# One wait less ahead of the load of expert 0's down weights, in a two-layer trunk step with a mixture of experts

## The chip, the cores and the metric

The kernel runs on one core of a Trainium2 chip. The metric is the device time of one execution in microseconds; of several executions the median is taken. Inside a core, TensorE (PE) multiplies matrices, VectorE (DVE) and ScalarE (ACT) work element by element, GpSimd (POOL) does small work and issues the indirect DMAs, and SyncE (SP) does nothing but wait and issue loads. All DMAs of a core, whoever issues them, are carried by its 16 DMA engines.

## What is computed

Two layers, each of attention (three groups of heads) and a mixture of experts, for 128 context tokens and 256 latent tokens, 384 in all, of width 1024. The change lies where the mixture of experts begins:

```python
def moe(h, w_router, b_router, w_gate, w_up, w_down):
    ...
    scores = jax.nn.sigmoid(jnp.einsum('nd,de->ne', t, w_router, ...))
    ...                                   # the best group of 4, then the top 2 in it
    hg = jnp.einsum('nd,edf->nef', t, w_gate)      # 16 experts, 1024 -> 512
    hu = jnp.einsum('nd,edf->nef', t, w_up)
    a = jax.nn.silu(hg) * hu * gate[..., None].astype(t.dtype)
    y = jnp.einsum('nef,efd->nd', a, w_down)       # 512 -> 1024
```

The kernel does not compute all 384 tokens for each of the 16 experts: it gathers the tokens that chose an expert, multiplies them with that expert's three matrices, and scatters the rows back.

## The kernel before

**Weights.** Every weight matrix of an expert (gate, up, down) is 2 MB in float32. SP loads them, in the order in which they are wanted, into a ring of six SBUF slots (`ring`). Each layer reuses the slots that held the attention weights and, last before the experts, chunks of the modulation matrix `w_ada`. In an expert phase SP's list is: gate 0 into slot 0, up 0 into slot 1, gate 1 into slot 2, up 1 into slot 3, down 0 into slot 4, gate 2 into slot 5, up 2 into slot 0 again, down 1 into slot 1, and so on, 48 loads in a layer. Gate 2 and what follows are read by number from `order`, a list of experts sorted by their token counts, which DVE writes in the router (L2398, semaphore `s_order`). `step(i, u)` (below) issues the three loads that go with expert 2i+1+u: its gate and up and the down matrix of the expert before it. Ahead of each load SP waits until the slot is free: the first time for the last reader of what stood in it (`before(slot)`, `is_filled`, L574), later for PE to have used up the expert's weights (`s_gd`, `s_gu`, `s_y`).

**Tokens.** In the router ACT writes the rows of the normalised activations to a scratch tensor in HBM (`hscr`, three DMAs of 512 KB from L1749). DVE makes the row numbers of the first two experts (`idx`, L2378), and POOL gathers their tokens from `hscr` (L2735), expert 0 first, then expert 1. PE turns expert 0's tokens (`tokens(0, ...)`, L1308), ACT and DVE split them into a high and a low part, and the matmuls of gate 0 start.

**Splitting the weights.** Weights in heavy experts are multiplied as a rounded high part and a remainder: ACT writes the high part (L1765), DVE the low part (L2437), and PE runs three matmuls per block (L1231, L1232, L1239). Half of the experts (those with few tokens) are "light" and are multiplied as they are (L1326, L1328, L1261). The loop over the experts is the same on every engine, in a fixed order per engine, so an engine that waits for a piece holds up all that stands behind it in its own list.

**The wait in question** stands in `step`, ahead of the down load of expert 0, so once in each layer: SP waits until the semaphore of the even gathers has risen by 16, that is, until expert 0's tokens lie in SBUF. It stands ahead of the check of slot 4, and gate 2 into slot 5 comes behind it on the same queue.

Of the kernel before, what the change touches and what calls it, by code (L numbers as in the profile page):

```python
# [263 lines left out]
def build(nc, A, C_dram, O):  # L264
    with ExitStack() as ctx:
# [389 lines left out]
        def gathers(l, p):  # L655

            return (s_g, [l * k for k in G_PASS]) if p == 0 else (s_gf[l, p], [0, 0])
# [25 lines left out]
        def _(sp):  # L683
# [4 lines left out]
            def chunk(l, k, parts):  # L688
                slot = k % SLOTS

                if k >= SLOTS:
                    is_filled(sp, last_reader(l, k - SLOTS))
                elif l > 0:
                    ring_after_experts(sp, slot, PASSES * (l - 1) + 1)
                for dst, src in parts(ring[slot][:]):
                    sp.dma_start(dst, src).then_inc(s_land[slot], 16)

            def cols(w, c, n):
                def parts(r):
                    return [(r[:, 0:KT * n].rearrange("p (k n) -> p k n", k=KT),  # L700
                             w.rearrange("(k p) n -> p k n", p=P)[:, :, c:c + n])]
                return parts

            def in_tail(l):

                w = A["w_in"][l].rearrange("(k p) n -> p k n", p=P)
                a = NA_IN + QR
                b = a + KR + RD + SH * HD

                def parts(r):  # L710
                    v = r[:, 0:KT * 416].rearrange("p (k n) -> p k n", k=KT)
                    return [(v[:, :, 0:KR + RD], w[:, :, a:a + KR + RD]), (v[:, :, KR + RD:416], w[:, :, b:b + 256])]
                return parts

            def in_swq(l):

                w = A["w_in"][l].rearrange("(k p) n -> p k n", p=P)
                a = NA_IN + QR + KR + RD

                def parts(r):  # L720
                    v = r[:, 0:KT * 384].rearrange("p (k h s d) -> p k h s d", k=KT, h=3, s=2)
                    return [(v[:, :, h, s, :], w[:, :, a + (3 * s + h) * HD:a + (3 * s + h + 1) * HD])
                            for h in range(3) for s in range(2)]
                return parts

            def out_cols(l, c):

                w = A["w_out"][l]
                a = 5 * P
                b = a + SH // 2 * HD  # L730

                def parts(r):
                    v = r.rearrange("p (k n) -> p k n", k=KT)
                    return [(v[:, 0:5, :], w[0:a].rearrange("(k p) n -> p k n", p=P)[:, :, c:c + 512])] + \
                           [(v[HD * s:HD * (s + 1), 5:8, :], w[r0:r0 + SH // 2 * HD].rearrange("(k p) n -> p k n", p=HD)[:, :, c:c + 512])
                            for s, r0 in enumerate((a, b))]
                return parts

            for l in range(DEPTH):
                w_in = (cols(A["w_in"][l], 0, 512), cols(A["w_in"][l], 512, 512), in_tail(l), in_swq(l))  # L740
                for k, (kind, *x) in enumerate(STREAM[l]):
                    if (l, k) == (0, len(ADA_FIRST) + 1):
                        sp.dma_start(cst[:, 2 * P:], C_dram[:, 2 * P:KEPT_W]).then_inc(s_const2, 16)
                        sp.dma_start(swaf, C_dram[:, KEPT_W:CONST_W]).then_inc(s_swaf, 16)
                    if kind in ("rows", "none"):
                        continue
                    if kind == "ada":
                        chunk(l, k, cols(A["w_ada"][x[0]], x[1] * 512, 512))
                    elif kind == "in":
                        chunk(l, k, w_in[x[0]])  # L750
                    else:
                        chunk(l, k, out_cols(l, x[0] * 512))

                def load(l, p, slot, use, w, e):
                    src = w[l, e] if isinstance(e, int) else w[l, bass.ds(e, 1)].rearrange("a p n -> (a p) n")
                    sp.dma_start(ring[slot][:], src).then_inc(moe_land(l, p, slot, 0)[0], 16)

                def stream(p):
                    n = PASSES * l + p

                    def before(slot):

                        if p == 0:
                            is_filled(sp, last_reader(l, MOE_AT[l] - SLOTS + slot))
                        else:
                            ring_after_experts(sp, slot, n)
                    before(0)
                    load(l, p, 0, 0, wg_d, 0)
                    before(1)
                    load(l, p, 1, 0, wu_d, 0)  # L770

                    def expert_at(e):

                        if p or (isinstance(e, int) and e < 2):
                            return e
                        at_e = order[0:1, e:e + 1] if isinstance(e, int) else order[0:1, bass.ds(e, 1)]
                        return sp.value_load(at_e, min_val=0, max_val=NE - 1)

                    def step(i, u):

                        e = 2 * i + 1 + u
                        if p == 0 and isinstance(i, int) and (i, u) == (0, 1):
                            sp.wait_ge(s_order, l + 1)
                        here, back_one = expert_at(e), expert_at(e - 1)
                        for kind, (w, s, back) in enumerate(((wg_d, s_gd, 1), (wu_d, s_gu, 1), (wd_d, s_y, 2))):
                            slot, use = place(u, kind)
                            if p == 0 and isinstance(i, int) and (e, kind) == (1, 2):
                                sp.wait_ge(gathers(l, 0)[0][0], gathers(l, 0)[1][0] + 16)
                            if isinstance(i, int) and i == 0 and use == 0:
                                before(slot)  # L790
                            elif isinstance(i, int) and i == 0:

                                sp.wait_ge((s_gd, s_gu)[slot], n * NE + 1)
                            else:
                                sp.wait_ge(s, e + n * NE - back)
                            load(l, p, slot, use, w, back_one if kind == 2 else here)
                    step(0, 0)
                    step(0, 1)
                    with sp.Fori(1, NE // 2 - 1) as i:
                        step(i, 0)  # L800
                        step(i, 1)
                    step(NE // 2 - 1, 0)
                    last_one = expert_at(NE - 1)
                    sp.wait_ge(s_gd, n * NE + NE - 1)
                    load(l, p, 5, 0, wd_d, last_one)
                    if p:

                        sp.wait_ge(s_y, (n + 1) * NE)

                stream(0)  # L810

                sp.wait_ge(s_cnt, l + 1)
                most = sp.value_load(cnti[0:1, 0:1], min_val=0, max_val=T)

                def rows_back(passes):

                    if passes == 1:
                        sp.wait_ge(s_gu, NE * PASSES * l + NE - 1)
                        sp.wait_ge(s_y, NE * PASSES * l + NE - 2)
                    else:  # L820
                        sp.wait_ge(s_y, NE * PASSES * (l + 1))
                        sp.wait_ge(s_further, (PASSES - 1) * (l + 1))
                    for k in range(2):
                        sp.wait_ge(s_sc[k], (l + 1) * SC_FIRST)
                    for t in range(NT):
                        sp.dma_start(yl[t], yscr.rearrange("(k t p) d -> t p k d", k=TOPK, p=P)[t]).then_inc(s_yl[t], 16)

                def skip_streams(p, many):
                    rows_back(p)
                    for s in s_land2:  # L830
                        wait(sp, s, 16 * (MOE_CH // SLOTS) * ((PASSES - 1) * l + p - 1))
                        for _ in range(many):
                            sp.sem_inc(s, 16 * MOE_CH // SLOTS)

                def stream_and_rows(p):
                    stream(p)
                    if p == PASSES - 1:
                        rows_back(PASSES)

                further_passes(sp, most, stream_and_rows, skip_streams)  # L840
# [1986 lines left out]
```

## Time and profile before

| | us |
|---|---|
| three runs | 1092.69, 1094.74, 1096.26 |
| median of the runs | 1094.74 |
| the profiled execution, its own time | 1095.41 |
| its span, first to last instruction | 1093.4 |
| mean granted TensorE clock over the span | 0.978 |

The profile's span is 2.0 us shorter than the time of that execution; the rest lies around the program. The profiled execution is 0.67 us above the median of the runs. PE is busy for 1008.0 us of the span (92%), DVE for 649.6 us, ACT for 534.3 us and POOL for 184.1 us; the queue that carries SP's loads moved 285.58 MB. Layer 0's expert phase lies at about 277 to 545 us of the span, layer 1's at about 794 to 1065 us.

Each row read from the trace below is a whole line of an answer. In a timeline a row gives start and duration of an instruction, the engine, the line of the kernel, what it writes and reads, and, in square brackets, how long the engine stood idle before it and what ended that.

### The profile page before, as it was taken

How to read it: one execution, taken by the hardware profiler on the slowest of the kernel's cores; microseconds unless marked ns; L12 is line 12 of the kernel's file. 1: busy time of each engine (PE TensorE's matmuls, PEld its weight loads, DVE VectorE, ACT ScalarE, POOL GpSimd, SP SyncE). 2: the span in 40 equal slices, each digit the busy share in tenths (PEclk: the TensorE clock that was granted, in tenths of full speed). 3: DMA queues.
4: the chain of work that ended last, by engine and by line, in shares of the span. 5: the costliest groups of instructions: out<-in, count | busy, mean ns of one | idle time of the engine just before them, and what ended most of it. 6: DMA issues, size and time to landing. Idle time of an engine off the chain costs nothing.

```text
span 1093.4 us, 15340 instructions
## 1 busy us (share of the span) xinstructions
PE 1008.0 (92%) x5607; PEld 699.0 (64%) x5607; DVE 649.6 (59%) x1135; ACT 534.3 (49%) x809; POOL 184.1 (17%) x184
## 2 busy tenths in 40 slices
PE   6999998897899999999999999789789999999987
PEld 4799454594686666665549975459368666666545
DVE  4355645667996454555345546775799644455534
ACT  2423554635575444555324356663646554445523
POOL 0226200150121111221040011000023111122002
PEclk8999999999899999999989999999989999999998
DMA  9997998347699999999699463002779999999961
GB/s 347 345 331 213 360 304 285 109 149 289 242 353 366 416 414 414 422 390 414 266 382 277 152 206 120 1 2 77 289 260 380 372 411 413 415 411 402 407 246 58
DMA packets 80895, 320.03 MB, mean 293 GB/s; under 512 B 20755, under 2 KB 25217, under 8 KB 68028
## 3 DMA queue, kind: packets, MB, share of 16 engines
q1 hardware_dynamic: 67232, 285.58, 68.7%
q0 software_dynamic: 12496, 30.37, 8.3%
q10 hardware_dynamic: 1100, 3.23, 0.7%
q8 instruction: 37, 0.61, 0.2%
q14 instruction: 30, 0.25, 0.1%
HBM read 304.38 MB, written 27.43 MB: 303 GB/s over the span
## 4 chain that ended last, share of the span: by engine, by line
PE 61%; DMA 14%; DVE 11%; ACT 6%; issue 5%; SPq 1%; POOL 0%; ACTq 0%; DVEq 0%; POOLq 0%
DMA ring<-in_w_down 12%; PE bank L1239 7%; PE bank L1231 6%; PE bank L1232 6%; PE bank L1326 4%; PE bank L947 3%; PE bank L951 3%; PE bank L944 3%; PE bank L1124 2%; PE bank L1138 2%; PE bank L1261 2%; ACT work L1705 2%; DVE ring_r L2437 2%; PE bank L921 2%; ACT work_r L1765 2%
## 5 line engine op out<-in xcount | busy, mean ns | idle before, releaser
L2437 DVE TENSOR_TENSOR ring_r<-ring,work_r 128x4096 fp32r<-128x4096 f32 x52 | 228.7, 4419 | 59.4 <-ACT work_r L1765 59.2
L1765 ACT ACTIVATE work_r<-ring 128x4096 fp32r<-128x4096 f32 x51 | 185.2, 3632 | 43.6 <-DMA ring<-in_w_down 18.9
L1231 PE MATMUL bank<-work_r 128*128 128x512 f32 x432 | 172.6, 399 | 6.1 <-DVE work_r L2453 5.1
L1232 PE MATMUL bank<-work_r 128*128 128x512 f32 x432 | 168.6, 390 | 0.0
L1239 PE MATMUL bank<-ring_r,work_r 128*128 128x512 f32 x432 | 112.0, 401 | 4.3 <-DVE ring_r L2437 4.3
L2735 POOL DMA_INDIRECT work<-hscr,idx x32 | 56.0, 1751 | 330.7 <-PE bank L1317 98.6
L1326 PE MATMUL bank<-ring,work 128*64 128x512 f32 x224 | 99.1, 595 | 0.0
L1328 PE MATMUL bank<-ring,work 128*64 128x512 f32 x224 | 99.1, 595 | 0.0
L1231 PEld LDWEIGHTS bank<-work_r 128*128 128x128 f32 x432 | 81.2, 188 | 26.6 <-issue 7.3
L1239 PEld LDWEIGHTS bank<-ring_r,work_r 128*128 128x128 f32 x432 | 79.2, 188 | 28.8 <-DVE ring_r L2437 11.6
L1232 PEld LDWEIGHTS bank<-work_r 128*128 128x128 f32 x432 | 81.2, 188 | 16.2
L2746 POOL DMA_INDIRECT yscr<-work,idx x28 | 39.1, 1396 | 187.6 <-ACT work L1831 121.1
L1326 PEld LDWEIGHTS bank<-ring,work 128*64 128x64 f32 x224 | 29.5, 137 | 57.7 <-issue 56.0
L1621 ACT ACTIVATE work_r<-ring 128x512 fp32r<-128x512 f32 (+1 forms) x48 | 28.8, 605 | 68.4 <-PE bank L951 68.3
L2089 DVE TENSOR_TENSOR ring_r<-ring,work_r 128x512 fp32r<-128x512 f32 (+1 forms) x48 | 33.1, 696 | 48.7 <-ACT work_r L1621 48.6
L2480 DVE TENSOR_TENSOR work_r<-bank,work_r 128x512 fp32r<-128x512 f32 x18 | 12.4, 691 | 81.2 <-ACT work_r L1817 81.2
L921 PE MATMUL bank<-ring,sil 128*32 128x512 f32 x384 | 52.0, 665 | 9.3 <-ACT work L1705 6.3
L1261 PE MATMUL bank<-ring,work 128*64 128x512 f32 x224 | 54.0, 627 | 6.6 <-issue 6.6
L1705 ACT ACTIVATE work<-bank,st 128x384 f32<-128x384 f32 (+1 forms) x96 | 47.9, 506 | 19.2 <-DVE st L2180 10.8
L2180 DVE TENSOR_REDUCE st<-bank 128x2 f32<-128x768 f32 (+1 forms) x48 | 37.3, 778 | 29.5 <-PE bank L1124 19.7
L1771 ACT ACTIVATE work<-bank 128x512 f32<-128x512 f32 x14 | 8.4, 598 | 79.2 <-PE bank L1317 79.2
L1124 PE MATMUL bank<-work 64*128 64x384 f32 (+3 forms) x192 | 45.6, 453 | 0.9 <-ACT work L1705 0.9
(307 smaller groups left out, 1743.4 us busy)
## 6 DMA issues: line engine op xcount, KB each, us to landing
ring<-in_w_gate SPq DMA_DIRECT2D x32, 2048.0 KB, 14.6
ring<-in_w_up SPq DMA_DIRECT2D x32, 2048.0 KB, 16.9
ring<-in_w_down SPq DMA_DIRECT2D x32, 2048.0 KB, 17.9
ring<-in_w_ada SPq DMA_DIRECT2D x24, 2048.0 KB, 11.2
ring<-in_w_in SPq DMA_DIRECT2D x4, 2048.0 KB, 19.0
yscr<-hT POOLq DMA_DIRECT2D x2, 3072.0 KB, 13.1
ring<-yscr SPq DMA_DIRECT2D x6, 1024.0 KB, 7.3
ring<-in_w_out SPq DMA_DIRECT2D x4, 1280.0 KB, 6.3
```

The costliest lines, as they stand in the source:

```text
L921: last = mm(b[32 * (k % 4):32 * (k % 4) + 32, :], sil32[:, k, :], w[:, k, :], start=(k < 4), stop=(k >= 4), skip_group_check=True)
L1124: last = mm(b[:, s, 0:n], lhs, rhs, start=True, stop=True)
L1231: mm(b[:], x_hi[:, k, :], hi[:, k, half, :], start=(k == 0), stop=False)
L1232: last = mm(b[:], x_lo[:, k, :], hi[:, k, half, :], start=False, stop=False)
L1239: last = mm(b[:], x_hi[:, k, :], lo[:, k, half, :], start=False, stop=(k == nk - 1))
L1261: last = mm(b[LS * h:LS * h + LS, :], aT[:, k, :], w[:, k, h, :], start=(k == 0), stop=(k == 3), skip_group_check=True)
L1326: up = mm(bG[0:LS, :], xs_l[:, k, :], wu[:, k, 0, :], start=(k == 0), stop=(k == KT - 1), skip_group_check=True)
L1328: gate = mm(bG[LS:P, :], xs_l[:, k, :], wg[:, k, 0, :], start=(k == 0), stop=(k == KT - 1), skip_group_check=True)
L1705: ins = A_(pr[(2 * i + s) % 6][:, 0:n], b[:, s], ACT.Exp, bias=st[:, r, 0, s:s + 1], accum_out=st[:, r, 1, s:s + 1])
L1765: A_(w_hi[:, slot % 2, :], ring[slot][:], ACT.Copy).then_inc(s_hi, 1 + behind)
L2437: tt(ring_r[slot][:], ring[slot][:], w_hi[:, slot % 2, :].bitcast(F32), ALU.subtract).then_inc(s_lo, 1 + behind)
L2735: g.indirect_dma_start(grow[rows, e % 2, :], None, hscr, bass.IndirectOffsetOnAxis(ap=idx[rows, e + 2, 0:1], axis=0), bounds_check=bound_h ...
```

## The change

The wait is taken out, in both layers. Nothing else differs: order of the loads, slots, and all other waits are the same.

```diff
@@ -784,8 +784,6 @@
                         here, back_one = expert_at(e), expert_at(e - 1)
                         for kind, (w, s, back) in enumerate(((wg_d, s_gd, 1), (wu_d, s_gu, 1), (wd_d, s_y, 2))):
                             slot, use = place(u, kind)
-                            if p == 0 and isinstance(i, int) and (e, kind) == (1, 2):
-                                sp.wait_ge(gathers(l, 0)[0][0], gathers(l, 0)[1][0] + 16)
                             if isinstance(i, int) and i == 0 and use == 0:
                                 before(slot)
                             elif isinstance(i, int) and i == 0:
```

With e = 1 and kind = 2 the load is `wd_d` of `back_one`, which is expert 0.

## Rows read from the trace of the kernel before

**Rows 1.** The page's part 4: the chain that ended last, by engine, by line.
```profile
PE 61%; DMA 14%; DVE 11%; ACT 6%; issue 5%; SPq 1%; POOL 0%; ACTq 0%; DVEq 0%; POOLq 0%
DMA ring<-in_w_down 12%; PE bank L1239 7%; PE bank L1231 6%; PE bank L1232 6%; PE bank L1326 4%; PE bank L947 3%; PE bank L951 3%; PE bank L944 3%; PE bank L1124 2%; PE bank L1138 2%; PE bank L1261 2%; ACT work L1705 2%; DVE ring_r L2437 2%; PE bank L921 2%; ACT work_r L1765 2%
```

**Rows 2.** Windows of layer 0: length, busy by engine, PE clock, DMA share, GB/s.
```profile
293.00:294.00 1.00, 1.00 (x9) 0.92 (x8) 0.86 (x6) 1.00 (x1) 0.00 (x0) 1.00 0.10 33
...
301.00:302.00 1.00, 1.00 (x6) 0.84 (x5) 1.00 (x1) 0.68 (x1) 1.00 (x1) 1.00 0.00 0
...
345.00:346.00 1.00, 1.00 (x10) 0.95 (x10) 1.00 (x1) 1.00 (x2) 0.00 (x0) 1.00 0.27 103
346.00:440.00 94.00, 94.00 (x438) 59.95 (x437) 48.58 (x31) 48.98 (x43) 14.90 (x13) 1.00 1.01 413
```

**Rows 3.** Windows of layer 1: the same columns.
```profile
817.00:818.00 1.00, 1.00 (x6) 0.82 (x5) 1.00 (x1) 1.00 (x1) 1.00 (x1) 1.00 0.04 16
```

**Rows 4.** Waits of SP's queue, 260:300 and 780:815: us in total, times, longest.
```profile
SPq L756 <- DMA work<-hscr,idx: 10.9, 1, 10.9
...
SPq L756 <- DMA work<-hscr,idx: 13.0, 1, 13.0
```

**Rows 5.** Timeline of SP: down 0, gate 2, up 2 (layer 0); down 0 (layer 1).
```profile
280.48 0.33 SPq L756 DMA_DIRECT2D ring<-in_w_down  x1
281.86 0.36 SPq L756 DMA_DIRECT2D ring<-in_w_gate  x1
293.46 0.34 SPq L756 DMA_DIRECT2D ring<-in_w_up  x1
...
798.33 0.33 SPq L756 DMA_DIRECT2D ring<-in_w_down  x1
```

**Rows 6.** Landing of one load with the DMA engines to itself, issued at 748.1.
```profile
DMA to landing us min/median/max: 7.8/7.8/7.8
```

**Rows 7.** Line L1749, the three writes of hscr: layer 0, then layer 1.
```profile
L1749 ACTq DMA_DIRECT2D hscr<-work x3: 327/350/362, 267.1 to 270.1; - x3
...
DMA to landing us min/median/max: 2.8/3.1/3.3
...
L1749 ACTq DMA_DIRECT2D hscr<-work x3: 327/328/1147, 782.9 to 786.7; - x3
...
DMA to landing us min/median/max: 3.0/4.1/4.3
```

**Rows 8.** Timeline of POOL: the first gather of layer 0, of layer 1.
```profile
277.07 1.10 POOL L2735 DMA_INDIRECT work<-hscr,idx  x1 [40.63 <-DVE idx L2378]
...
794.12 1.09 POOL L2735 DMA_INDIRECT work<-hscr,idx  x1 [63.04 <-issue]
```

**Rows 9.** Timeline of DVE: order (layer 0); row numbers, order (layer 1).
```profile
278.49 0.19 DVE L2398 CAST order<-ranked 128x14 int32<-128x14 f32 x1
...
793.14 0.17 DVE L2378 TENSOR_SCALAR idx<-slotf 128x4 int32<-128x4 f32 x1
...
795.60 0.17 DVE L2398 CAST order<-ranked 128x14 int32<-128x14 f32 x1
```

**Rows 10.** Landing, line L2735: first gather layer 0, layer 1; second, layer 0; all 32.
```profile
DMA to landing us min/median/max: 3.4/3.4/3.4
...
DMA to landing us min/median/max: 4.2/4.2/4.2
...
DMA to landing us min/median/max: 4.4/4.4/4.4
...
DMA to landing us min/median/max: 3.4/9.0/14.7
```

**Rows 11.** Timeline of PE: expert 0's tokens turned, layer 0 and layer 1.
```profile
281.99 1.92 PE L1308 MATMUL bank<-cst,work 128*128 128x128 f32 x8
...
800.61 1.04 PE L1308 MATMUL bank<-cst,work 128*128 128x128 f32 x8
```

**Rows 12.** Timeline of ACT: the first use of down 0, layer 0.
```profile
307.63 3.63 ACT L1765 ACTIVATE work_r<-ring 128x4096 fp32r<-128x4096 f32 x1
```

## The prediction

> **What bounds the kernel now.** I began with the chain that ended last, because the change touches loads only: if loads sit on that chain, an earlier load may pay. PE has 61% of it, and one kind of load, the down weights, has 12%, the largest single line [rows 1]. So loads matter somewhere; the question is whether they matter where this load stands. Next I read the windows of the expert phase. In layer 0, from 346 to 440 us, the 16 DMA engines are full (share 1.01, 413 GB/s) and PE is busy for all 94.00 us [rows 2]: both run flat out. But before that there are stretches in which the DMA engines have nothing left to carry: share 0.10 in 293 to 294, 0.00 in 301 to 302 and 0.27 in 345 to 346 [rows 2]; in layer 1, 0.04 in 817 to 818 [rows 3]. PE is busy for the whole of each of these windows. What the reader should see: the stream of loads runs dry several times after the place of the change, while PE goes on working. A stream that runs dry forgets when its earlier parts were delivered. Last I read the waits of SP's queue: the gather held it for 10.9 us in layer 0 and 13.0 us in layer 1, once each [rows 4]. That is the wait that goes, 23.9 us in total, and it is a wait of SP alone.
>
> **The change part by part.**
>
> *Down 0 moves forward.* It is issued at 280.48 and at 798.33 [rows 5]. Without the wait it goes when slot 4 is free, which is where the wait for the gather began to count: 280.48 - 10.9 = 269.6 in layer 0, 798.33 - 13.0 = 785.3 in layer 1. A load that has the engines to itself lands 7.8 us after its issue [rows 6], so at 277.4 and 793.1. What runs beside it are the writes of hscr, the last issued at 270.1 and 786.7 [rows 7]; each is 0.52 MB, 1.3 us at 413 GB/s [rows 2]. At most two of them are still under way, so down 0 lands between 277.4 and 280.0, and between 793.1 and 795.7.
>
> *What that buys.* The first instruction that reads down 0 is ACT's split at 307.63 in layer 0, and no wait stands before it in its row [rows 12]; ACT starts it when its own work before it is through. Down 0 had been issued 27 us earlier and has 27 us to land even now. Nothing is bought here: 0 us. The cover is those 27 us, against 7.8 us that a load needs; if the cover were gone, the worth would be the transfer, up to 5.1 us (2.1 MB at 413 GB/s).
>
> *Gate 2 moves forward a little.* It stands behind down 0 and needs `order`, which is written at 278.49 + 0.19 = 278.68 in layer 0 and 795.60 + 0.17 = 795.77 in layer 1 [rows 9]. Between down 0 and gate 2 on SP lie 281.86 - 280.48 = 1.38 us [rows 5], of which 0.33 is down 0's own issue, so some 1.05 us go into reading the expert's number. Gate 2 then goes at about 279.7 (2.2 us earlier) and, by the same distance, at about 796.8. It is used after down 0, so it too was early enough: 0 us.
>
> *All the loads behind these do not move.* Up 2 is issued at 293.46 [rows 5] into slot 0, which PE must first have used up. The DMA engines stand nearly still in 293 to 294 [rows 2], so up 2 meets an empty stream before and after the change, and from it on every load has its old issue time. The transfer of down 0 is taken out of the stretch between 280.48 and 293.46 and put before it; what it leaves behind is a longer hole ahead of up 2. What is late next is still PE.
>
> *What stands in the way of the moved load: the writes of hscr.* The first gather reads what they write. In layer 0 the last write lands at 270.1 + 3.3 = 273.4 at the latest, the gather starts at 277.07 and names DVE's row numbers as what it waited for [rows 7, 8]: 3.7 us to spare. In layer 1 it lands at 786.7 + 4.3 = 791.0 at the latest, the row numbers are there at 793.14 + 0.17 = 793.31 [rows 7, 9]: 2.3 us to spare. If the write and down 0 share the engines evenly, the write takes 1.3 us longer: covered. If the whole of down 0 went ahead of it, 5.1 us longer, the gather would start 1.4 us late in layer 0 and 2.8 us late in layer 1; the slack that follows (next paragraph) leaves 0 and 0.5 us of it. Bounds 0 and +0.5 us; I take 0, because the write and the load are different queues and only one of the two is 7.8 us long.
>
> *The issue of the writes on ACT.* One of the three issues in layer 1 took 1.147 us where the others took 0.33 [rows 7]; I can't tell from the trace why. Should down 0's issue at 785.3 slow the write at 786.7 in the same way, ACT is 0.8 us late once. Bounds from 0 to +0.8 us; I take 0. A gain is excluded, since nothing is taken from ACT's list.
>
> *The first gather itself.* It starts at 277.07 and 794.12 [rows 8] and lands 3.4 and 4.2 us later [rows 10], at 280.5 and 798.3. PE turns the tokens at 281.99 and 800.61 [rows 11], in both layers without idle time of its own named in the row. So the gather may land 1.5 us later in layer 0 and 2.3 us later in layer 1 before PE sees it. What is new beside it: the tail of down 0, which is over by 280.0 at the latest in layer 0 and by 795.7 in layer 1, and in layer 1 the first packets of gate 2, issued at about 796.8. The nearest row for a gather with a load beside it is the second gather of layer 0, which runs while down 0 starts: 4.4 us [rows 10], 1.0 us more than the first. The far end is the median of all 32 gathers, 9.0 us [rows 10], most of which run with the engines full. By the near row the delay is 1.0 us and covered; by the far end it costs 286.1 - 281.99 = 4.1 us and 803.1 - 800.61 = 2.5 us. I take the near row, 0 us, because down 0 is all but over when the gather begins.
>
> A rule speaks against the change here. The rows show a gather at 3.4 to 4.4 us in quiet engines and 9.0 us in the median. The Trainium skill (DMA: Bandwidth & Descriptors, section "Issuing engines are not separate DMA queues") says that transfers of all issuers run on the same 16 engines and interleave, so SP's load takes bandwidth from POOL's gather although the queues differ; this trace agrees as far as the 4.4 against 3.4 us go. By the rule alone the sum would rise by what the gather loses beyond its slack, which is the slower rival below.
>
> *Sum.* 0 + 0 + 0 + 0 us, with +0.5 + 0.8 us of small bounds and +6.6 us at the far end of the gather, nothing below zero except by the rival that follows. Against the profiled execution: 1095.41 + 0 = 1095.41. That execution is 0.67 us above the median of the runs, so the median I expect is 1094.7.
>
> **The rivals.**
>
> *Faster: the load stream is one queue, and 2.1 MB taken out of its busy part shortens it.* For: down loads are the largest line of the chain [rows 1], and from 346 us on the engines are full [rows 2]. If the stream were full from 281 us on, each layer would end 5.1 us earlier, 10.2 us in total: 1094.7 - 10.2 = 1084.5. Against: the three dry stretches in layer 0 and the one in layer 1 [rows 2, 3]; any lead is lost at the first of them. The Trainium skill (Perfetto Trace Analysis, section "Optimization Strategy") advises to look for the gaps on the most contended engine and to let what they wait for start sooner, which is just what this change does to the DMA engines; by that rule the gain would come, and the rows of the dry stretches speak against it here. Chance 0.05.
>
> *Slower: the first gather lands late.* The place is PE's turn of expert 0's tokens; it decides from the point at which the gather lands after 281.99 in layer 0 and 800.61 in layer 1. All later loads are issued when PE has used slots up, so a late PE makes a late stream, and the delay goes through to the end. Price at the median gather: 4.1 + 2.5 = 6.6 us, 1101.3. For: the wait kept every load off the engines just while this gather ran, and the gather's packets are few and needed to the last. Against: down 0 has 7.5 us (277.07 - 269.6) and 8.8 us (794.12 - 785.3) ahead of the gather, about what a load needs [rows 6]. Chance 0.10, half of it for a smaller loss of 1 to 4 us.
>
> *The change doesn't do what it says.* If something else holds SP at the same place (slot 4, or `order`, should it be read ahead of down 0), down 0 keeps its time. The split of SP's wait speaks against it: 10.9 and 13.0 us are put to the gather alone [rows 4]. The time would be 1094.7 as well. Chance 0.05, and it counts as no change.
>
> **How the numbers follow.** A measurement of this kernel can tell about 0.3%, 3.3 us, from no change; the three runs lie within 3.6 us. Forecast (no change because the moved transfer was off the chain): 0.80; with the idle change 0.85 in all, of which I give 0.05 to the two sides for noise and for the small bounds. Within 0.3%: 0.80. Faster: 0.05 + 0.02 = 0.07. Slower: 0.10 + 0.03 = 0.13. The likeliest time is 1094.7. The range takes the noise of the runs on the lower side, 1091.0, and on the upper side the small bounds and the smaller half of the late gather, 1099.5; the full price of either rival lies outside, about 1 in 10 together.
>
> **What would show each step.** In the profile of the changed kernel SP should issue down 0 at about 269.6 and 785.3 and gate 2 at about 279.7 and 796.8, and up 2 still at about 293.5; the wait for the gather should be gone from SP's list. The DMA share should rise in 271 to 278 and in 787 to 794, fall to nothing in about 287 to 294, and be as before from there on. The first gathers should land before 282.0 and 800.6, and L1308 should start within 0.3 us of its old times. The prediction is wrong if PE's first expert starts later (the gather, or the writes ahead of it), or if, with the same start, the stream from 302 us on runs ahead of the old one.

## The result, and the profile after

The median rose from 1094.6 (now of four runs) to 1106.56 us (1106.07 to 1107.51). The ratio is 1.0108, with a 95% interval from 1.0093 to 1.0123: 12 us slower, where I had forecast no change in a range from 1091.0 to 1099.5. The profiled execution took 1106.07 us; its span is 1104.0 us, 10.6 us more than before, at a mean clock of 0.975.

The moved loads did what the prediction said. The timeline of SP, after (down 0, gate 2, up 2 in both layers; it answers [rows 5]):

```profile
267.84 0.33 SPq L756 DMA_DIRECT2D ring<-in_w_down  x1
278.03 0.36 SPq L756 DMA_DIRECT2D ring<-in_w_gate  x1
297.42 0.34 SPq L756 DMA_DIRECT2D ring<-in_w_up  x1
...
787.72 0.33 SPq L756 DMA_DIRECT2D ring<-in_w_down  x1
798.12 0.35 SPq L756 DMA_DIRECT2D ring<-in_w_gate  x1
818.76 0.34 SPq L756 DMA_DIRECT2D ring<-in_w_up  x1
```

To read these against before, the drift of the execution has to be taken off. Up 1 is the last load ahead of the change. Its rows, and that of up 2 in layer 1 before; first after, then before:

```profile
253.47 0.33 SPq L756 DMA_DIRECT2D ring<-in_w_up  x1
...
772.13 0.33 SPq L756 DMA_DIRECT2D ring<-in_w_up  x1
```

```profile
255.14 0.33 SPq L756 DMA_DIRECT2D ring<-in_w_up  x1
...
769.72 0.33 SPq L756 DMA_DIRECT2D ring<-in_w_up  x1
...
809.96 0.34 SPq L756 DMA_DIRECT2D ring<-in_w_up  x1
```

Up 1 is issued 1.67 us earlier than before in layer 0 and 2.41 us later in layer 1. Up 2 is issued 297.42 - 293.46 = 3.96 us later in layer 0 and 818.76 - 809.96 = 8.80 us later in layer 1. So between up 1 and up 2 the kernel loses 3.96 + 1.67 = **5.6 us** in layer 0 and 8.80 - 2.41 = **6.4 us** in layer 1, 12.0 us in all. Every load of layer 0 from up 2 to the last ones near 512 us is 3.8 to 4.0 us late: the loss is made in these 40 us and is then carried along, neither given back nor added to; in layer 1 the loads from up 2 to 1028 us are 8.2 to 8.9 us late in the same way. (The difference of two up 2's, less that of two up 1's, is what "loss" means in the table below.)

In that stretch three things are late, one behind the other. The third write of hscr, after (groups by line, from its issue to its landing; answers [rows 7]; layer 0, then layer 1):

```profile
L1747 ACTq DMA_DIRECT2D hscr<-work x1: 326/326/326, 268.5 to 268.5; - x1
DMA to landing us min/median/max: 9.6/9.6/9.6
...
L1747 ACTq DMA_DIRECT2D hscr<-work x1: 326/326/326, 788.3 to 788.3; - x1
DMA to landing us min/median/max: 9.1/9.1/9.1
```

It is issued 0.6 us behind down 0 and takes 9.6 and 9.1 us, where it took 3.3 and 3.0 [rows 7]. The first gather of POOL and its landing, after (answers [rows 8, 10]):

```profile
278.91 1.56 POOL L2733 DMA_INDIRECT work<-hscr,idx  x1 [44.15 <-DMA hscr<-work]
DMA to landing us min/median/max: 7.6/7.6/7.6
...
797.68 1.09 POOL L2733 DMA_INDIRECT work<-hscr,idx  x1 [64.20 <-DMA hscr<-work]
DMA to landing us min/median/max: 9.4/9.4/9.4
```

The releaser in brackets has changed: the gather no longer starts on DVE's row numbers but on the write. The row numbers after (layer 0, layer 1), and before (layer 0; layer 1 is in [rows 9]):

```profile
274.37 0.17 DVE L2376 TENSOR_SCALAR idx<-slotf 128x4 int32<-128x4 f32 x1
...
794.68 0.17 DVE L2376 TENSOR_SCALAR idx<-slotf 128x4 int32<-128x4 f32 x1
```

```profile
276.02 0.17 DVE L2378 TENSOR_SCALAR idx<-slotf 128x4 int32<-128x4 f32 x1
```

They are there at 274.54 and 794.85, so the gather starts 4.4 and 2.8 us behind them, against 0.9 us (from 276.19) and 0.8 us before [rows 8, 9]. By then gate 2 is under way (278.03) or about to be (798.12), and the gather lands 7.6 and 9.4 us later instead of 3.4 and 4.2 [rows 10]: at 286.5 and 807.1, some 0.2 and 0.6 us after gate 2 itself (landing 8.3 and 8.4 us behind its issue). And PE, after (answers [rows 11]):

```profile
286.66 1.95 PE L1306 MATMUL bank<-cst,work 128*128 128x128 f32 x8 [7.45 <-DMA work<-hscr,idx]
807.16 1.97 PE L1306 MATMUL bank<-cst,work 128*128 128x128 f32 x8 [4.44 <-DMA work<-hscr,idx]
```

PE stands idle for 7.45 and 4.44 us for the gather, in front of expert 0's tokens, where its rows of before named no idle time. Less the drift, the turn of the tokens is 6.3 us late in layer 0 (286.66 - 281.99 + 1.67) and 4.1 us in layer 1 (807.16 - 800.61 - 2.41). In layer 1 another 2.3 us come before up 2. The windows there show the granted clock (the column behind the five engines), first after, then before:

```profile
802.00:806.00 4.00, 0.71 (x3) 0.00 (x1) 2.02 (x4) 0.00 (x0) 0.00 (x0) 0.93 0.87 360
806.00:810.00 4.00, 2.84 (x11) 2.15 (x12) 0.21 (x1) 0.84 (x2) 0.00 (x0) 0.50 0.12 50
810.00:814.00 4.00, 4.00 (x13) 2.69 (x12) 4.00 (x4) 0.25 (x1) 0.00 (x0) 0.67 0.01 4
```

```profile
802.00:806.00 4.00, 3.82 (x18) 2.60 (x17) 4.00 (x5) 0.78 (x2) 0.00 (x0) 1.00 1.00 426
806.00:810.00 4.00, 4.00 (x52) 3.29 (x51) 4.00 (x1) 2.86 (x1) 0.00 (x0) 1.00 0.94 397
```

Behind its idle stretch PE works at 0.50, the lower of its two levels (1.2 GHz), until past 810; before, it had the full clock here. That fits the 2.3 us; no run tested the clock by itself.

**Why the write is late.** The records of the DMA queues say it (queue, packets, MB, share of the 16 engines; q1 carries SP's loads, q10 ACT's writes), after, first in 270.3 to 272.7 us, then in 273 to 275.5:

```profile
q1 hardware_dynamic: 56, 0.92, 103.3%
...
q1 hardware_dynamic: 47, 0.77, 85.2%
q10 hardware_dynamic: 47, 0.19, 18.7%
```

Two things are to be seen. First, the write starts late. It was issued at 268.46, yet in this window of 2.4 us the load has the engines to itself (no packet of q10). By the records of single packets the write's first 4 KB row goes 4.5 us behind its issue, and 4.2 us in layer 1; in the kernel before it goes 0.8 us behind the issue in both. What holds it is open. Second, from 273 us on both queues get 47 packets in 2.5 us, one for one; but a load's packet is 16 KB and a packet of the write is one row of 4 KB, so the load gets four bytes for each byte of the write. The Trainium skill (DMA: Bandwidth & Descriptors, section "Queues, rings and completion order") says that each engine goes round between the queues it has work for, packet by packet. From 273 us on this trace agrees, 47 to 47 (the packets counted here are single rows); before that it shows 56 packets of the load to none of the write. Of the 6.3 us by which the write lands later than before in layer 0, some 3.7 us are the late start, and the rest, some 2.6 us, comes behind it, where the write takes turns with the longer packets.

The gather starts late in the same way. The queues after in layer 0 (q0 carries POOL's gathers), first in 279 to 283.8 us, then in 283.8 to 286.5:

```profile
q1 hardware_dynamic: 103, 1.69, 98.8%
...
q0 software_dynamic: 277, 0.26, 28.0%
```

Its first packet goes 4.9 us behind its start at 278.91 (5.2 us in layer 1), when most of gate 2 has been carried; in the kernel before it goes 1.7 us behind the start in both layers. So 3.2 and 3.5 of the 4.2 and 5.2 us by which the gather takes longer are the late start.

### The profile page after: what moved, and what is told of

It is laid out like the page before. It is cut to its first block, busy times and chain, and to the rows that moved or that the text cites. A ratio compares the mean times of both kernels' runs of the same rounds, so it can differ in the third digit from the quotient of the medians.

```text
span 1104.0 us, 15336 instructions
## 1 busy us (share of the span) xinstructions
PE 1006.0 (91%) x5605; PEld 697.4 (63%) x5607; DVE 649.0 (59%) x1135; ACT 534.4 (48%) x809; POOL 183.6 (17%) x184
## 4 chain that ended last, share of the span: by engine, by line
PE 60%; DMA 16%; issue 9%; DVE 7%; ACT 6%; SPq 1%; ACTq 0%; DVEq 0%; POOLq 0%
DMA ring<-in_w_down 12%; PE bank L1237 7%; PE bank L1229 6%; PE bank L1230 6%; PE bank L1324 5%; PE bank L1259 3%; PE bank L945 3%; PE bank L949 3%; PE bank L942 3%; PE bank L1122 2%; PE bank L1136 2%; ACT work L1703 2%; ACT work_r L1763 2%; DVE ring_r L2435 2%; PE bank L1014 2%
## 5 line engine op out<-in xcount | busy, mean ns | idle before, releaser
L2478 DVE TENSOR_TENSOR work_r<-bank,work_r 128x512 fp32r<-128x512 f32 x18 | 12.4, 691 | 81.2 <-ACT work_r L1815 81.2
L919 PE MATMUL bank<-ring,sil 128*32 128x512 f32 x384 | 49.6, 639 | 10.9 <-ACT work L1703 6.4
```

The costliest lines, as they stand in the source:

```text
L919: last = mm(b[32 * (k % 4):32 * (k % 4) + 32, :], sil32[:, k, :], w[:, k, :], start=(k < 4), stop=(k >= 4), skip_group_check=True)
```

## The experiments

The theory after reading: the third write is late because it takes turns with long packets (the turn theory; the late starts above are no part of it); the gather is then late and meets gate 2; PE's idle time is carried to the end (the chain theory). Rivals: that the early start of the loads in itself, whatever becomes of the gather, costs the time (a worse order in the stream, or loads beside other work); that the late write alone is the whole of it; that the meeting of gather and gate 2 alone is. In the kernels below, the same lines stand 2 to 6 lines lower down than in the one after.

| kernel | third write lands after, us | gather lands after, us | PE idle for the gather, us | loss, us | ratio to before |
|---|---|---|---|---|---|
| before | 3.3 / 3.0 | 3.4 / 4.2 | none / none | - | 1 |
| after | 9.6 / 9.1 | 7.6 / 9.4 | 7.45 / 4.44 | 5.6 / 6.4 | 1.0108 |
| gate 2 held | 9.2 / 9.8 | 3.6 / 4.2 | 2.89 / none | 1.8 / -0.2 | 1.0022 |
| behind the writes | 3.3 / 4.1 | 5.0 / 5.8 | 0.43 / none | 0.2 / -0.4 | 1.0004 |
| short packets | 7.0 / 8.4 | 3.3 / 4.3 | none / none | 0.0 / -0.6 | 0.9998 |
| at the row numbers | 3.3 / 3.0 | 10.2 / 11.3 | 6.41 / 4.60 | 6.1 / 6.6 | 1.0074 |
| the same, short packets | 3.3 / 3.0 | 7.9 / 8.1 | 2.86 / 0.88 | 2.1 / 2.3 | 1.0029 |

(layer 0 / layer 1, of each kernel's profiled execution; ratios from all its timed executions, against executions of the kernel before taken beside them.) A loss in the table is that of one execution, and of the stretch from up 1 to up 2 alone. The profiled executions of "behind the writes" (1101.92 us) and of "the same, short packets" (1102.89 us) lie some 6 and 4 us above their kernel's median by what they lost elsewhere, and a layer that still has its old wait can be 1.6 us off (last section). The ratios carry the verdicts.

**Gate 2 held.** Down 0 is as early as in the kernel after; the wait for the gather stands one load later, ahead of gate 2.

```diff
-                            if p == 0 and isinstance(i, int) and (e, kind) == (1, 2):
+                            if p == 0 and isinstance(i, int) and (e, kind) == (2, 0):
                                 sp.wait_ge(gathers(l, 0)[0][0], gathers(l, 0)[1][0] + 16)
```

> Edit: down 0 goes when slot 4 is free, as in the changed kernel; the wait for expert 0's gather stands ahead of gate 2 instead. The changed kernel has two things that are late: the third write of hscr (landing 9.6 us after its issue instead of 3.3 us) and, because the gather then starts late, a gather that meets gate 2 (7.6 us instead of 3.4 us). Chain theory (the late write starts it, gate 2 makes it dear): the write stays late, so the gather starts 3.5 us later than the row numbers allow in layer 0 and 2.0 us in layer 1, but lands in 3.4 to 4.2 us again; less the slack of 1.5 and 2.3 us that is +2 us in layer 0 and 0 in layer 1, so 1.002 of the time of before. Gate theory (only the meeting of gather and gate 2 costs, whoever started it): 1.000. Write theory (the late write alone costs): the whole loss, 1.011.

Measured: 1.0022 [1.0008, 1.0036], 1097.3 us. The first gather and PE's turn, in layer 0 and layer 1:

```profile
277.98 1.32 POOL L2735 DMA_INDIRECT work<-hscr,idx  x1 [42.76 <-DMA hscr<-work]
...
281.69 1.95 PE L1308 MATMUL bank<-cst,work 128*128 128x128 f32 x8 [2.89 <-DMA work<-hscr,idx]
...
794.79 1.09 POOL L2735 DMA_INDIRECT work<-hscr,idx  x1 [64.92 <-DMA hscr<-work]
...
799.08 1.16 PE L1308 MATMUL bank<-cst,work 128*128 128x128 f32 x8
```

The write is as late as in the kernel after (9.2 and 9.8 us) and the gather starts on it, but it lands 3.6 and 4.2 us later, as in quiet engines. So the late write alone costs 1.8 us in layer 0 and nothing in layer 1, and the meeting with gate 2, with what follows from it, makes the rest of the 12.0 us: some 10. That is the chain theory's 1.002; the write theory's 1.011 and the gate theory's 1.000 lie outside the interval.

**Behind the writes.** Down 0 waits for the writes of hscr instead of the gather; gate 2 is free.

```diff
                             if p == 0 and isinstance(i, int) and (e, kind) == (1, 2):
-                                sp.wait_ge(gathers(l, 0)[0][0], gathers(l, 0)[1][0] + 16)
+                                sp.wait_ge(s_hscr, 16 * NT * (l + 1))
```

> Edit: down 0 waits until the three writes of hscr have landed instead of the gather; gate 2 as in the changed kernel. Down 0 is then issued at about 273.5 and 790, still 7 to 8 us earlier than in the kernel before, and runs while the gather starts at 277.07 and 794.12. Chain theory: the write lands in 3 us, the gather is issued on time and ahead of gate 2, and shares the engines with the second half of down 0 only; it lands with down 0 at 281.3 to 282 and at about 798 to 799, within the slack: 1.000 to 1.001. Gate theory: gate 2 still goes at about 279.7 and 796.8, so some of the loss stays, 1.003 to 1.006. Any theory in which an earlier down 0 as such is worth time: below 0.998.

Measured: 1.0004 [0.9985, 1.0022], 1095.69 us. Layer 0, down 0 on SP, the first gather, PE's turn:

```profile
275.39 0.33 SPq L756 DMA_DIRECT2D ring<-in_w_down  x1
...
278.99 1.10 POOL L2735 DMA_INDIRECT work<-hscr,idx  x1 [40.89 <-DVE idx L2378]
...
284.09 1.13 PE L1308 MATMUL bank<-cst,work 128*128 128x128 f32 x8 [0.43 <-DMA work<-hscr,idx]
```

The gather is released by the row numbers again. It has the rest of down 0 beside it and lands 5.0 and 5.8 us later, which PE's slack all but covers (0.43 us idle). Down 0 is 6.8 and 8.3 us earlier than before once the drift is taken off, and the time is the same within 0.2%: the early load costs nothing by itself, and buys nothing. The gate theory (1.003 to 1.006) is out.

**Short packets.** No wait, as in the kernel after; down 0 is one DMA still, but each partition's row is described as four runs of 4 KB, last to first, so that they are not merged into one of 16 KB.

```diff
+                    if p == 0 and w is wd_d and isinstance(e, int) and e == 0:
+                        v4 = [x.rearrange("p (b n) -> p b n", b=4)[:, ::-1, :] for x in (ring[slot][:], src)]
+                        sp.dma_start(v4[0], v4[1]).then_inc(moe_land(l, p, slot, 0)[0], 16)
+                        return
...
-                            if p == 0 and isinstance(i, int) and (e, kind) == (1, 2):
-                                sp.wait_ge(gathers(l, 0)[0][0], gathers(l, 0)[1][0] + 16)
```

> Edit: the changed kernel, no wait, but the one DMA of down 0 is described as four runs of 4 KB per partition, walked from the last to the first, instead of one run of 16 KB; same bytes, same place, same time of issue, one DMA. Turn theory (each DMA engine takes a packet from each queue in turn, and a packet of down 0 is 16 KB against the 4 KB of a row of hscr, so the write gets a fifth of the engine): with 4 KB against 4 KB the third write lands 4.5 to 6 us after its issue instead of 9.6, the gather is issued within 1 us of its old place, ahead of gate 2, and the loss is gone: 1.000 to 1.002. Issue-order theory (what was issued first is carried first, whatever its packets): the write still lands with down 0, 9 to 10 us after its issue, and the loss stays, 1.010 to 1.012.

Measured: 0.9998 [0.9975, 1.0022], 1095.59 us. The whole loss is gone, with down 0 as early as in the kernel after. The queues in 272 to 274.5 us, down 0 on SP, the first gather and PE's turn in layer 0:

```profile
q1 hardware_dynamic: 131, 0.54, 52.3%
q10 hardware_dynamic: 125, 0.51, 49.3%
...
267.73 0.63 SPq L758 DMA_DIRECT2D ring<-in_w_down  x1
...
276.18 1.10 POOL L2737 DMA_INDIRECT work<-hscr,idx  x1 [40.51 <-DMA hscr<-work]
...
280.22 1.91 PE L1310 MATMUL bank<-cst,work 128*128 128x128 f32 x8
```

Again one for one (131 to 125 packets), and now the bytes are even too: 0.54 to 0.51 MB, where it was 0.77 to 0.19. The write lands after 7.0 us instead of 9.6, the gather starts 2.7 us earlier than in the kernel after and lands in 3.3 us, its tokens ahead of PE's need. The loss is gone as the turn theory had it, and the issue-order theory's 1.010 to 1.012 is out. What differs from the kernel after is the length of the load's packets, and with it the order of the runs within a row and the time of its issue on SP (0.63 instead of 0.33 us).

The write itself, though, is later than the turn theory's 4.5 to 6 us: 7.0 us, and 8.4 in layer 1. Most of what is left over 3.3 us is the late start again, which short packets cure only in part: its packets begin some 3 us behind its issue, against 0.8 in the kernel before and 4.5 in the kernel after. In layer 1 the write is only 0.7 us earlier than in the kernel after, and that is enough. The gather starts 1.17 us ahead of gate 2's issue (792.89, 794.06) and lands in 4.3 us; in the kernel after it started 0.44 us ahead (797.68, 798.12) and took 9.4 us. Between these two runs, less than a microsecond in the gather's lead over gate 2 decides the loss.

**One layer alone.** The wait goes in layer 1 and stays in layer 0.

```diff
-                            if p == 0 and isinstance(i, int) and (e, kind) == (1, 2):
+                            if p == 0 and l == 0 and isinstance(i, int) and (e, kind) == (1, 2):
```

> Edit: the wait stands in layer 0 and is missing in layer 1. The two traces put the loss of the changed kernel at 5.6 us in layer 0 and 6.4 us in layer 1 (the shift of the loads from up 2 on against the loads before it). If the two are independent, this kernel loses 6.4 us: 1.006 (1.005 to 1.007). If the loss of one layer is partly given back behind it, or the second depends on the first, it differs from that by more than 2 us.

Measured: 1.0071 [1.0046, 1.0096], 1103.37 us. Layer 1 loses 5.4 us with PE idle for 4.33 us, against 6.4 and 4.44 in the kernel after: layer 1 loses by itself, and the ratio fits the 6.4 us within its interval. The profiled execution is also longer in layer 0, with the wait in place, by some 1.6 us at up 2 and 3.3 us by 319 us; the last section says what its rows show.

**At the row numbers.** Down 0 waits until the row numbers are ready, just ahead of the gather; gate 2 is free. The writes are then done, and the gather starts on time, with down 0 just ahead of it and gate 2 behind.

```diff
                             if p == 0 and isinstance(i, int) and (e, kind) == (1, 2):
-                                sp.wait_ge(gathers(l, 0)[0][0], gathers(l, 0)[1][0] + 16)
+                                sp.wait_ge(s_slot, NG * n + 1)
```

> Edit: down 0 waits for the row numbers of the first two experts (what POOL waits for too) instead of the gather, so SP issues it at about 276.3 and 793.4, some 1.9 us before the gather's descriptors are out; gate 2 as in the changed kernel. The writes of hscr have long landed. This measures what a 2 MB load just ahead of the gather costs, without a late write. Turn theory: the gather lands with down 0, at 284 to 284.5 in layer 0 and 801.2 to 801.8 in layer 1, 3.5 to 4 us later than in the kernel before; less the slack of 1.5 and 2.3 us that is +2 to +2.5 us and +1 to +1.5 us: 1.003 (1.002 to 1.0045). Write theory (only the late write costs): 1.000.

Measured: 1.0074 [1.0050, 1.0099], 1104.54 us; slower, as expected, but by more than twice as much. The second kernel of this pair is the same with down 0 in short packets, as above:

> Edit: as the kernel in which down 0 waits for the row numbers, but its DMA is described as four runs of 4 KB per partition. Turn theory: a gathered row of 4 KB now takes turns with packets of 4 KB, and an engine has only one or two rows to fetch; the gather lands 4.5 to 6 us after its issue, at 281.5 to 283 in layer 0 and 798.5 to 800 in layer 1, most of the loss of the twin is gone: 1.000 to 1.0015. If the gather is held by what was issued first, whatever the packets, it equals its twin, 1.002 to 1.0045.

Measured: 1.0029 [1.0015, 1.0043], 1098.84 us. PE's turn in both layers, first with long packets, then with short ones:

```profile
285.81 1.94 PE L1308 MATMUL bank<-cst,work 128*128 128x128 f32 x8 [6.41 <-DMA work<-hscr,idx]
807.93 1.97 PE L1308 MATMUL bank<-cst,work 128*128 128x128 f32 x8 [4.60 <-DMA work<-hscr,idx]
```

```profile
284.13 1.94 PE L1312 MATMUL bank<-cst,work 128*128 128x128 f32 x8 [2.86 <-DMA work<-hscr,idx]
805.44 1.97 PE L1312 MATMUL bank<-cst,work 128*128 128x128 f32 x8 [0.88 <-DMA work<-hscr,idx]
```

With long packets the gather is issued 0.85 us behind down 0 (275.49, 274.64) and lands at 285.7, past down 0's landing at 283.0 as well; gate 2 (278.12) had joined. I had sized the meeting with down 0 alone and left gate 2 out; no run held gate 2 here. With down 0's packets in quarters the gather takes 7.9 and 8.1 us instead of 10.2 and 11.3, and the stretch loses 2.1 and 2.3 us instead of 6.1 and 6.6. That is less help than I expected (4.5 to 6 us, 1.000 to 1.0015). Gate 2 keeps its long packets, which may be one reason, but no run shortened them. Another is in the rows. The queues from the gather's start in layer 0, in 275.5 to 280 us with long packets, then in 276.2 to 280.6 with short ones:

```profile
q1 hardware_dynamic: 92, 1.51, 99.8%
...
q1 hardware_dynamic: 299, 1.22, 84.2%
```

In neither does the gather have a packet there: its first goes 4.6 us behind its start in both kernels, against 1.7 us in the kernel before. Short packets shorten only what comes behind the late start. So long packets are one part of what the gather suffers from and the late start is another, as with the write. This pair loses without any late write; the kernel with gate 2 held loses little with one. Each does harm only through the time at which PE gets its tokens.

**Later still.** The wait stays, and down 0 also waits until PE has turned expert 0's tokens. This tests the cover that the prediction gave to the load: 27 us in hand, so 3 us more of waiting should cost nothing.

```diff
                                 sp.wait_ge(gathers(l, 0)[0][0], gathers(l, 0)[1][0] + 16)
+                                sp.wait_ge(s_xt, n * NE + 1)
```

> Edit: the wait of the kernel before is kept and made longer: down 0 also waits until PE has turned expert 0's tokens, so it and gate 2 go 3 to 4 us later than in the kernel before (about 284 and 801.8). The prediction held that down 0 has some 27 us in hand, so that neither an earlier nor a later load is worth anything: 1.000 (0.999 to 1.001). If the lead of these loads did count, 3.5 us in each layer would show as 1.003 to 1.006.

Measured: 1.0029 [1.0009, 1.0050], 1099.23 us; expected was no change. Down 0 goes at 283.24 and 801.39, 2.3 and 3.0 us later than before without the drift. Layer 0 costs 0.1 us, as expected, and at up 2 of layer 1 nothing has been lost either. Then, between the loads at 828.76 and 839.41, 4.1 us go. The gather of the third expert's tokens (issued 14 us behind the delayed load; start and landing), and PE's turn of its tokens:

```profile
L2736 POOL DMA_INDIRECT work<-hscr,idx x1: 4933/4933/4933, 815.2 to 815.2; - x1
DMA to landing us min/median/max: 16.0/16.0/16.0
...
831.24 1.97 PE L1309 MATMUL bank<-cst,work 128*128 128x128 f32 x8 [2.51 <-DMA work<-hscr,idx]
```

The landing of the same gather in the kernel before (issued at 815.6):

```profile
DMA to landing us min/median/max: 12.5/12.5/12.5
```

It looks like the same event one place further on. Down 0 and gate 2 late pushed the stream into the stretch from 812 to 818 us, where the DMA share is 0.99 instead of 0.74; the gather issued there took 16.0 us instead of 12.5, PE stood for it, and its clock fell (0.72 in 830 to 836, against 1.00). The load that I had called covered was; what was not covered is a gather that meets the loads behind it. That this gather was held by the later loads is read from one trace; no run took those loads away, and the kernel with the change in layer 1 alone shows such a gather in layer 0 without any moved load (last section). That the delay is what made it late rests on the ratio, whose interval begins at 1.0009.

None of these kernels is faster than the one before. Where the gathers are on time, the time is that of before.

## Why the prediction was wrong

**Right.** What SP does: down 0 was to go at about 269.6 and 785.3, and went at 269.5 (267.84 + 1.67) and 785.3 (787.72 - 2.41). Gate 2 was to go at 279.7 and 796.8 and went at 279.7 and 795.7. That an earlier load buys nothing: behind the writes and in short packets down 0 came 6.8 and 11.0 us earlier in layer 0 at ratios of 1.0004 and 0.9998, which also excludes the faster rival's 10.2 us. (The reason given, that the stream runs dry behind it, fits [rows 2, 3]; no run tested it.) That the place of the danger is PE's turn of expert 0's tokens, that a late PE makes a late stream, and that this goes through to the end: of the 5.6 us lost by 297 us, 5.4 are still there at 512 us. That the change does what it says.

**The first step that failed is the writes of hscr**, taken at 0 us with 0.5 us as the bound. I had two sizes for their delay: 1.3 us if the write and the load share evenly, which I took, and 5.1 us if the whole load goes first, my far bound. It was 6.3 us in layer 0 and 6.1 us in layer 1, above the far bound. The write's first packet went 4.5 us behind its issue instead of 0.8, which no row of before could show and which is the larger part. Behind it the sharing was not even by bytes: the two queues took turns by packets, and these are 4 KB and 16 KB. The reason given, that queue and queue differ, is no reason for even shares. By itself the late write cost 1.8 us in layer 0 and nothing in layer 1 (gate 2 held).

**The second step that failed, and the dearer one, is the first gather**, taken at 0 us by the near row of 4.4 us. It took 7.6 and 9.4 us, and the meeting with gate 2 makes some 10 of the 12.0 us. The failure is in adding up. The write's delay was priced with a gather that takes its old 3.4 and 4.2 us, and the gather's delay with a start that is on time. I wrote that down 0 is all but over when the gather begins, and that was so (it landed at 277.6, the gather began at 278.9). But I had myself put gate 2 at 279.7, 2.6 us behind a gather that begins at 277.07; a gather that begins 3.5 us late stands behind gate 2. In layer 1 it was 2.0 us late and 0.44 us ahead of gate 2's issue, which was not enough. So the two terms are not separate: the first decides whether the second is near its near end or its far one. The median of 9.0 us [rows 10] was the fitting row, for 7.6 and 9.4 us; 3.4 to 4.4 us was the row of quiet engines.

**The rival** of the late gather was right in place and mechanism, and its price of 6.6 us was about half of the 12.0 us, since it left out that the gather itself is issued late, behind the write, and the clock. At 0.10 its chance was too low. The rule of the Trainium skill that I weighed there (DMA: Bandwidth & Descriptors, section "Issuing engines are not separate DMA queues"), that transfers of all issuers interleave on the same engines, bore it out: beside gate 2 the gather took 7.6 and 9.4 us, against 3.4 and 4.2.

**The cover of 27 us** that I gave down 0 holds for down 0 alone. In the profiled execution with the later load, 4.1 us were lost in layer 1 by way of a gather 14 us further on; over all its executions the ratio is 1.0029.

## What to carry to other kernels

A wait on a load queue can be there for a small transfer on another queue: before taking it out, list the small transfers that the moved load, and the loads behind it, will meet, and ask of each how much slack its reader has. A 512 KB transfer in 4 KB rows, issued 0.6 us behind a 2 MB one in 16 KB rows, took three times its time (9.6 against 3.3 us). It was late in two ways: its first packet came late (4.5 us behind the issue instead of 0.8), and from then on the engines were shared by packets, not by bytes. Equal packets cured the second and little of the first, but that, or letting the small one finish first, took the loss away (0.9998 and 1.0004 against 1.0108). Delays in a chain must be followed through one after the other, since each decides what the next one meets; priced one by one they seemed covered, together they cost 12 us.

## What was not expected of the hardware

- A packet of the load of 16 KB and a packet of the write of 4 KB count the same in the turns: 47 to 47 in 2.5 us.
- The write, issued 0.6 us behind a load, put no packet on the engines in 270.3 to 272.7 us, while the load filled them (103.3%). It began 4.5 us behind its issue, with short packets of the load some 3 us, and 0.8 us in quiet engines. A first gather that started within 1 us of a load's issue began 4.6 to 5.2 us behind its start, with long packets and with short ones, against 1.7 us in the kernel before. Why is open.
- A gather with two loads beside it takes 10.2 and 11.3 us, against 3.4 and 4.2 us in quiet engines. That of the third expert, a larger one (4.9 us on POOL instead of 1.1), took 12.5 us in layer 1 of the kernel before and 16.0 where the stream was fuller.
- The same code can meet the low clock at another moment. In the kernel with the change in layer 1 alone, layer 0 has the old wait, and yet 284 to 288 us ran at 0.57 there, where the kernel before had 0.92, and up 2 came 1.6 us later. The windows, first 284 to 288 us of that kernel, then two of the one before:

```profile
284.00:288.00 4.00, 4.00 (x13) 2.48 (x12) 4.00 (x4) 0.00 (x0) 0.00 (x0) 0.57 1.04 438
```

```profile
280.00:284.00 4.00, 3.22 (x14) 2.42 (x12) 4.00 (x7) 2.46 (x3) 0.00 (x0) 0.50 0.78 221
284.00:288.00 4.00, 2.56 (x12) 1.76 (x13) 3.93 (x9) 2.83 (x3) 0.00 (x0) 0.92 1.02 434
```

PE was at the low level in both, before in 280 to 284 and there in 284 to 288, where it has work for all 4.00 us. That the clock is the cause of the 1.6 us fits these rows; no run tested it.
- In the same layer, with its old wait, the gather of the third expert took 14.9 us where the kernel before took 12.4, and PE stood for it. PE's turn of its tokens there:

```profile
313.86 1.16 PE L1308 MATMUL bank<-cst,work 128*128 128x128 f32 x8 [1.33 <-DMA work<-hscr,idx]
```

By 319 us the layer has lost 3.3 us in all. So much can come and go in a single execution, which is why the verdicts above rest on the timed ratios.
